# A hybrid decoder layer on one core: the softmax division of the prompt attention moves from ScalarE to VectorE, and the state space output matrix is loaded ahead of the value store

## The reference

```python
h = _rmsnorm(x, g_norm)
u, q, k, v = jnp.split(h @ w_in, ...)          # 1024 columns each; rotary on q, k
# S5: complex diagonal states, y = Re(C x) + D u, GELU, GLU
y = jnp.einsum('gpn,bsgn->bsgp', c_c, xs).real + d_skip * uf
# attention of the prompt, 8 heads of 128: three dilated branches, merged
p = jnp.exp(scores - m); l = jnp.sum(p, axis=-1, keepdims=True)
o = jnp.einsum('brnhqk,brnkhc->brnqhc', p / l, vb)
# RMSNorm of both halves, output projection, router, 2 of 32 SwiGLU experts, final RMSNorm
```

## Time and profile before

| | |
|---|---|
| median of 3 runs | 2065.87 us (2064.89 to 2072.14) |
| the profiled execution, its own time | 2076.94 us |
| its span | 2075.1 us |
| busy in the span: PE, PEld, DVE, ACT, POOL | 1787.2, 1116.2, 661.0, 265.7, 285.8 us |
| attention of the prompt, first score to first lag product | 489.88 to 569.92 us |

### The profile page before, as it was taken

The page is one execution under the profiler, slowest core; times in us unless marked ns, Lnnn a source line. Parts: engine busy times, 40 slices in busy tenths (PEclk is TensorE's granted clock), DMA queues, the critical chain, the costliest instruction groups (busy, mean ns, idle before and its releaser), DMA issues.

```text
span 2075.1 us, 22180 instructions
## 1 busy us (share of the span) xinstructions
PE 1787.2 (86%) x8780; PEld 1116.2 (54%) x8780; DVE 661.0 (32%) x1275; ACT 265.7 (13%) x524; POOL 285.8 (14%) x188
## 2 busy tenths in 40 slices
PE   8999999998698999995979898989877878788760
PEld 7878888885377888883334343434332323223220
DVE  6900999641454400006412212121111111111116
ACT  3003111005532111011000000000000000000002
POOL 0652222104801000001100101010000000000000
PEclk9999999999899999997989999999999899899985
DMA  5254222357744143216899999999999999999947
GB/s 233 82 138 107 69 80 101 127 194 97 3 164 184 61 163 147 97 62 261 336 409 410 409 411 405 403 401 386 389 406 391 410 398 411 402 410 405 409 169 284
DMA packets 90885, 540.67 MB, mean 261 GB/s; under 512 B 28248, under 2 KB 41048, under 8 KB 44664
## 3 DMA queue, kind: packets, MB, share of 16 engines
q1 hardware_dynamic: 77792, 515.95, 66.4%
q0 software_dynamic: 5632, 17.12, 2.4%
q10 hardware_dynamic: 7376, 6.39, 1.1%
HBM read 521.91 MB, written 31.98 MB: 267 GB/s over the span
## 4 chain that ended last, share of the span: by engine, by line
PE 56%; DMA 28%; DVE 6%; POOL 3%; ACT 3%; issue 1%; ACTq 1%; SPq 1%; POOLq 0%; DVEq 0%
PE psum L597 29%; DMA arena<-w_up_in 25%; PE psum L895 8%; PE psum L930 6%; PE psum L888 3%; PE psum L891 3%; PE psum L871 1%; ACTq L988 1%; PE psum L694 1%; SPq L512 1%; PE psum L897 1%; DMA arena<-y_rows 1%; DMA arena<-v_cache_in 1%; PE psum L637 1%; PE psum L806 1%
## 5 line engine op out<-in xcount | busy, mean ns | idle before, releaser
L597 PE MATMUL psum<-arena 128*128 128x260 f32 x3328 | 743.5, 387 | 15.0 <-DMA arena<-w_in_in 8.3
L597 PEld LDWEIGHTS psum<-arena 128*128 128x128 f32 x3328 | 639.2, 192 | 116.2 <-DMA arena<-w_in_in 8.3
L895 PE MATMUL psum<-arena 128*64 128x512 f32 x896 | 439.1, 649 | 115.6 <-DMA arena<-w_up_in 114.8
L897 PE MATMUL psum<-arena 128*64 128x512 f32 x896 | 440.0, 650 | 0.0
L895 PEld LDWEIGHTS psum<-arena 128*64 128x64 f32 x896 | 129.5, 149 | 379.1 <-issue 378.0
L930 PE MATMUL psum<-arena 128*64 128x512 f32 (+1 forms) x1024 | 259.7, 604 | 17.6 <-ACT arena L1132 17.4
L930 PEld LDWEIGHTS psum<-arena 128*64 128x64 f32 (+1 forms) x1024 | 87.2, 145 | 166.9 <-issue 143.4
L1246 POOL DMA_INDIRECT y_rows<-arena x32 | 37.0, 1156 | 932.9 <-DVE arena L1690 552.2
L1679 DVE TENSOR_TENSOR arena<-arena,psum 64x512 f32<-64x512 f32 x28 | 19.4, 692 | 457.8 <-ACT arena L1129 457.8
L897 PEld LDWEIGHTS psum<-arena 128*64 128x64 f32 x896 | 129.4, 149 | 15.3 <-issue 15.3
L1690 DVE COPY arena<-psum 64x512 f32<-64x512 f32 (+1 forms) x64 | 43.7, 688 | 256.5 <-PE psum L930 255.6
(11 more groups left out here) (320 smaller groups left out, 1315.5 us busy)
## 6 DMA issues: line engine op xcount, KB each, us to landing
arena<-w_gate_in SPq DMA_DIRECT2D x64, 2048.0 KB, 39.0
arena<-w_up_in SPq DMA_DIRECT2D x64, 2048.0 KB, 43.0
arena<-w_down_in SPq DMA_DIRECT2D x64, 2048.0 KB, 42.2
arena<-w_in_in SPq DMA_DIRECT2D x32, 1024.0 KB, 4.8
arena<-w_out_in SPq DMA_DIRECT2D x16, 1024.0 KB, 4.7
arena<-k_cache_in SPq DMA_DIRECT2D x8, 1024.0 KB, 6.8
arena<-v_cache_in SPq DMA_DIRECT2D x8, 1024.0 KB, 4.9
arena<-y_rows SPq DMA_DIRECT2D x4, 2048.0 KB, 19.7
```

The source lines that it names most:

```text
L597: last = mm(banks[:, h, :], w(kk), rhs(kk)[:, HALF * h:HALF * (h + 1)], start=(kk == first), stop=(kk == kn - 1 and stop))
L895: lastg = mm(ps[0:SLIM, 2, :], xt[:, 8 * hf + kk, :], wg[:, kk, :], start=(hf == 0 and kk == 0), stop=(hf == 1 and kk == 7))
L897: lastu = mm(ps[SLIM:P, 2, :], xt[:, 8 * hf + kk, :], wu[:, kk, :], start=(hf == 0 and kk == 0), stop=(hf == 1 and kk == 7))
```

## The change

The division leaves ScalarE's stream. VectorE's `invert` becomes `divide`: it takes the reciprocal, waits for its own result, and multiplies the row in place with a `tensor_scalar` (times the reciprocal, plus 0.0) that also writes the sum of the row into a column of the statistics that nothing reads at that stage, and releases `s_pr` to TensorE. The loop of VectorE is divide(a), mask(a + 3), scale_b. On SP the load of `ssm_c`, with its two waits, moves from behind the router constants to between the key store and the value store's wait. The ring of half blocks stays as it is.

```diff
             sp.dma_start(t["k_out"], k).then_inc(s_kout, 16)
+            sp.wait_ge(s_proj, 32)
+            sp.wait_ge(s_state, 1)
+            sp.dma_start(cw[:, 0], t["ssm_c"]).then_inc(s_c, 16)
             sp.wait_ge(s_rope, 24)
             sp.dma_start(t["v_out"], v).then_inc(s_vout, 16)
...
-            sp.wait_ge(s_proj, 32)
-            sp.wait_ge(s_state, 1)
-            sp.dma_start(cw[:, 0], t["ssm_c"]).then_inc(s_c, 16)
             sp.wait_ge(s_vout, 16)
...
-            def divide(a):
-                act.wait_ge(s_rl, a + 1)
-                w = P * (a % 4 + 1)
-                A(sc[a % 4][:, 0:w], sc[a % 4][:, 0:w], ACT.Copy, scale=stat[:, 36 + a % 4:37 + a % 4]).then_inc(s_pr, 1)
-
...
             for a in range(4 * NH):
-                divide(a)
                 if a + 2 < 4 * NH:
                     exps(a + 2)
                 turned(a)
...
-            def invert(a):
+            def divide(a):
+                w = P * (a % 4 + 1)
+                inverse = stat[:, 36 + a % 4:37 + a % 4]
                 dve.wait_ge(s_exp, a + 1)
-                dve.reciprocal(stat[:, 36 + a % 4:37 + a % 4], stat[:, 32 + a % 4:33 + a % 4]).then_inc(s_rl, 1)
+                dve.reciprocal(inverse, stat[:, 32 + a % 4:33 + a % 4]).then_inc(s_rl, 1)
+                dve.wait_ge(s_rl, a + 1)
+                ts(sc[a % 4][:, 0:w], sc[a % 4][:, 0:w], inverse, 0.0, ALU.mult, ALU.add,
+                   accum_out=stat[:, 40 + a % 4:41 + a % 4]).then_inc(s_pr, 1)
...
             for a in range(4 * NH):
-                invert(a)
+                divide(a)
                 if a + 3 < 4 * NH:
                     mask(a + 3)
                 scale_b(a - 4 * NH + 14)
```

## The result

The changed kernel took 2054.3 us (median of 11 runs, 2049.71 to 2060.05). The kernel before, run beside it on the same chip, took 2069.16 (11 runs, 2063.18 to 2077.0). The ratio is 0.992, with a 95% interval of 0.9906 to 0.9935: 14.9 us less, or 13.4 to 19.5 by the ends of the interval. The microseconds forecast, 2054.4, and those measured agree better than the reasoning deserves. The forecast took 11.5 off the median of three runs, 2065.87, and the median of more runs of the same kernel is 3.3 higher. So the gain was about 3 us larger than forecast. The profiled execution of the changed kernel took 2054.3 with a span of 2052.5.

The account below looks back on a forecast made before the run. ScalarE was taken to set the attention's pace. Heads 0 to 3 gain 7.6 us, the rest 3.7 to 6.0; 11.5 taken off the median 2065.87 gives 2054.4, range 2050.5 to 2064 (without rivals 2052 to 2057).

Parts of the forecast that it names:

- The head: Attention, heads 0 to 3: a period of 6.50 us instead of 8.56, VectorE hidden under TensorE by 0.12 us.
- rival 3: VectorE bounds by more than counted, through dearer divisions, hand-overs or B operations: gain 6 to 9 us, about 2058.5; chance 0.12.
- head 0: First head of the attention, which has its start to get through: gain 1.4 us, between 0 and 2.06.
- The stretch of the B operations: Heads 4 to 6, seven B scalings on VectorE: six gaps take in divisions, 2.9 us, growing 20.06 to 23.0.
- What follows the stretch: Up to the weighing of head 6: three reciprocals and divisions, two masks, the last turn and its copy, 4.1 us.
- The last head: End of attention: 5.65 us, since it makes no scores for a next head; its weighing 2.3 or 4.6 us.
- Attention: The whole attention stage ends 10.8 to 13.6 us earlier, at 556.3 to 559.1; 11.5 was taken.
- The move: Output matrix loaded before the value store: lands at 489, GpSimd ends at 550 to 557; gains nothing by itself.
- The relay: Whole kernel: each stage waits for the one ahead, so microseconds won in the attention should reach the end whole.
- The first: Rival: each attention division waits for a GpSimd instruction, up to 2.15 us; 2086, or about 2068 with half; chance 0.13.
- The second: Rival: GpSimd's chain ends the attention, its matrix late or chain slowed 6 us; gain 8.3 us, 2057.6; chance 0.09.

Follow-up runs that it names:

- the repeat: The changed kernel run once more, nothing altered: 2056.3 us, ratio 0.9928 to the kernel before.
- the four executions: Traces with the division on VectorE and no extra work: the division alone (2063.39 us), the changed kernel (2054.3) and the same unaltered twice more (2056.3, 2056.0).
- the two repeats: The changed kernel run twice more, nothing altered: 2056.3 us, ratio 0.9928, and 2056.0 us, ratio 0.9924 to the kernel before.

## Why the prediction was right, and where it was off

**The head** held. Counted from the scores after a weighing (498.60), the last turn starts at 2.97 and its 0.62 end at 3.59, then 0.69 and 2.26: 6.54, forecast 6.50. The division was sized 0.05 short, and VectorE still ended 0.10 ahead of TensorE (501.47 and 501.57), forecast 0.12. The thin margin was right in size and did not matter: rival 3 fell for heads 0 to 3. From first score to the weighing of head 3 the gain is 6.8 to 7.1 (before 524.76 - 489.88 = 34.9; now 515.97 - 487.86 = 28.1 and, in the repeat, 517.82 - 490.04 = 27.8), forecast 7.6: 3 x 2.02 from the periods, and 0.7 to 1.0 from head 0, where I had 1.4.

**The stretch of the B operations is the term that was mis-sized.** The step that failed is "2.9, all of it on the path, since VectorE is the bound there". VectorE was busy for 19.93 of the 20.10 us then, but part of its busy time was waiting, inside the records of the B operations: they take 1.22 us, and the copy 0.69, without GpSimd's products, and took 1.8 to 2.7 beside them. The work besides them did grow as forecast, from 20.06 - 16.54 = 3.5 us to 19.74 - 12.83 = 6.9, 3.4 for 2.9; and the B operations shrank by 3.7, since a division that does not wait for GpSimd now fills time in which they would have waited. So the stretch took 19.74, not 23.0; over the four executions the divisions cost 18.5 - 17.7 = 0.9 on the mean, and up to 3 in one of them, when a turn is missed. The Trainium skill ("SBUF — State Buffer", SBUF: two separate sides) says that of an operation of VectorE with two SBUF inputs and one of GpSimd that reads SBUF the first to start has the port for its whole length; the trace agrees (1.08 us after the product's end, 2.22 after the B operation's). I had cited the rule against the division and had not read it for the B operations, to which it applied already before the change.

**What follows the stretch** took back part of that. From the end of the last B operation (539.90) to the weighing of head 6 (545.95) I had 4.1; it took 6.05. The windows of the changed kernel over three weighings (duration; busy time and count of PE, PEld, DVE, ACT, POOL; granted clock; DMA share; GB/s) show it:

```profile
536.89:541.52 4.63, 4.63 (x9) 2.81 (x10) 3.50 (x10) 0.54 (x2) 4.55 (x2) 0.50 0.90 8
545.95:548.37 2.42, 2.42 (x10) 1.62 (x11) 1.41 (x8) 0.54 (x2) 2.34 (x2) 1.00 0.00 0
551.88:555.86 3.98, 3.98 (x9) 2.19 (x9) 0.00 (x0) 0.00 (x0) 0.00 (x0) 0.58 0.00 0
```

The weighing of head 5 ran at the lower level, a granted clock of 0.50, after TensorE had idled 1.90 and 1.48 us for divisions, and VectorE's next mask waited for it. With the division alone TensorE idled 1.91 and 1.04 there, the same weighing took 2.42 at a granted clock of 1.00, and this piece 4.15. The last head took 5.93, forecast 5.65, its weighing 3.98 in a range of 2.3 to 4.6. From the weighing of head 3 to the lag product the pieces are 4.19 + 19.74 + 6.05 + 5.93 + 3.98 = 39.9, in the forecast's 39.2 to 41.5: two errors of opposite sign, and so luck. In the two repeats the same sum is 40.3 and 42.3, once inside and once above.

**Attention** as a whole, first score to lag product, went from 80.04 to 68.00, 68.10 and 70.20: 9.8 to 12.0 less. I took 11.5 and gave 10.8 to 13.6. The lag product came at 555.86, a little ahead of the 556.3 to 559.1 forecast, also because the first score did, at 487.86 instead of 489.88; that is this one execution (488.8 to 491.6 in all others), in which the transposes ahead of it took 3.71 instead of 5.38 us. It is no part of the change.

**The move** came out as argued: 487.77 in place of about 489, the end at 550.28 in place of 550 to 557, hidden under the attention's end, worth nothing alone and about 7 us behind the division. No transfer behind it was late: the load of B went out at 492.63, 0.6 later than before.

**The surplus** of about 3 us lies behind the attention, where I had no term. From the lag product to the first down product of the experts (L930) it was 988.07 - 569.92 = 418.2 before and 418.7 with the move alone; it is 414.1, 416.6 and 414.0 in the three executions of the changed kernel, 1.6 to 4.6 less. The lag products have 0.6 of it (3.7 for 4.26). The rest is spread over the samples' attention, the output projection and the stage before L930. In the eight other executions with the division on VectorE this piece is 415.3 to 419.4, so part of the surplus may be scatter; its cause stays open. Behind L930 the executions differ by up to 8 us whatever the kernel (1079 to 1087 to the end of the span). The relay held: L930 starts 13 to 18 us earlier.

**The rivals.** The first did not happen, and the run without a sum shows that its price, at half the wait, was nearly right. The second needs the move undone, and then gives its 8.3 at the lag product. The third was right on the place, heads 4 to 6, and wrong on the sign.

## What to carry to other kernels

A busy engine is not a sum of work: where an operation takes longer beside another engine than alone, new work that does not share the conflict can go into its waits for nothing, until a turn is missed. Ask of every long operation what it takes alone before adding to the queue that it bounds. And when a queue is relieved, look for the next release in line before counting the gain: half of this one hung on a load whose late issue had cost nothing before.

## What the runs showed of the hardware that I had not expected

- The division that also writes a sum takes 0.75 us for 512 columns, with GpSimd's products and without them. The plain one takes 0.49 after GpSimd's end and up to 2.37 beside it. The form that is dearer by itself is the one that is cheaper here. The Trainium skill ("VectorE: DVE Perf Modes", The perf-mode tier table) counts the plain float32 form among the faster two-port ones, and these rows agree.
- The wait is mutual: a GpSimd product takes 1.9 to 2.4 us where no B operation lies beside it, and mostly 2.8 to 3.2 between two of them.
- The same attention code took 17.0 to 20.7 us from the first B operation to the last in four executions. The first B operation took 1.73 to 3.15 us in them, by where it met GpSimd's chain, and in the longest the weighing of head 4 ran at a granted clock of 0.50 instead of 0.58 to 0.62. That these two make the whole spread is not shown.
